# A ConvFFN loop on one NeuronCore: another division of the eight PSUM banks, and another order of VectorE's sums and taps

## The chip, the cores and the metric

The kernel runs on one NeuronCore of a Trainium2 chip. The metric is the device time of one execution in microseconds. Inputs are float32; products on TensorE are made in three passes (high x high, high x low, low x high) so that they keep nearly float32 precision.

## The reference

A two-layer encoder over 1024 tokens of width 1024. Each layer has an attention part (MLA in layer 0, differential attention in layer 1) and then the ConvFFN that the change is about:

```python
def conv_ffn(h, w_up, conv_w, conv_b, w_down):
    u = h @ w_up                       # 1024 x 5632
    u = causal depthwise conv of width 3 over tokens (u) + conv_b
    gate, val = split(u, 2)            # 2816 each
    return (silu(gate) * val) @ w_down
```

The hidden width 2816 is 22 tiles of 128 rows. For every tile there is a gate tile and a value tile of `u` (128 x 1024 tokens), and the down product adds its share to all 8 output tiles.

## The kernel before

The engines run their own instruction lists and meet at semaphores that only count up. `ffn(layer)` exists once per engine.

**One iteration n of the loop (n = 2 to 21; HT = 22, PLAIN = 2).** The gate and the value tile n, each 1024 x 1024 x 128, are made with a Winograd form of the 2x2 block product: seven products P1 to P7 of half size instead of eight. Each product is four steps of three matmuls (L1112 to L1114) into one PSUM bank (128 x 512 float32); a tile pair of the down product, `down(n, f)` (L1117), is six matmuls (L1130 to L1132) into two banks. TensorE's order comes from `tensor_steps` (L73): P1 P6 P2 P5 P7 P4, down tile 0 of n-1, P3, down tiles 1 to 7 of n-1. The first two hidden tiles (n = 0, 1) are made in the plain way, gate in banks 0 and 1, value in banks 2 and 3.

**PSUM.** There are 8 banks. Products of n >= 2 go round banks 0 to 3 (`up_bank`, L535), down tiles alternate between banks 4, 5 and 6, 7 (L1128, L1825). `bank_free` (L1088) makes a product wait until the product that used its bank four products ago has been read: P1 by ScalarE's `bank_copy` (L1191), each other one by the VectorE sum that `RESULT_OF` (L67) names, P7 by C22 and U3. A down tile waits for the sum of the tile two back (`acc_done`, L1124).

**VectorE** (DVE). `result` (L1788) makes the sums of the Winograd form (128 x 512, one input in PSUM): U2 from P6, C11 from P2, W from P5, C22 and U3 from P7, C21 from P4, C12 from P3; C21 completes the value tile, C12 the gate tile (both in `cx`, double buffered). `conv_tile(n, v)` (L1803) adds the two older taps of the convolution (v = 0 gate, v = 1 value) behind ScalarE's `tap` (L1424), which does the newest tap and the bias: two operations of 128 x 1023 and 128 x 1022 with both tensors in SBUF (L1807, L1810). `product` (L1813) multiplies gate and value after ScalarE's Silu (`gate_and_split`, L1430), `hid_tail` (L1818) makes the low part of the result for TensorE, and `add` (L1823) adds one down tile to the accumulator `a`. The order in one iteration:

```python
U2(n); conv_tile(n-1, 1); product(n-1); C11; hid_tail(n-1); W; C22; U3; C21
add(n-1, 0); C12; add(n-1, 1..7); conv_tile(n, 0)
```

**ScalarE** (ACT), in order: `bank_copy(n)`, Silu and high part of n-1, the value's tap (after C21), the gate's tap (after C12 and `hid_tail(n-1)`).

**GpSimd** (POOL) prepares the weights: nine items an iteration (G1 S2 G2 S1 S3 V2 d1 S4 d2, `weight_items`, L89), each a cast (L786) and a subtraction (L788) of 128 x 512, and four weight sums (L797 to L805). The items live in a ring of five slots; `plan_ring` (L118) gives each item the slot that comes free first by the order of TensorE's steps, and the item waits for the step that frees it. SP loads the raw weights: `load_ffn` of V waits for item V2, of G for S4, of D for d2.

Around the start of each FFN (n = 2) P1 and P2 stand ahead of the eight down tiles of n = 0 and wait for the taps of plain tile 1 (gate, value), because those still read the banks.

Of the kernel before, what the change touches and what calls it, by code (L numbers as in the profile page):

```python
# [29 lines left out]
KT = D // P  # L30
# [4 lines left out]
HT = DFF // P  # L35
# [32 lines left out]
PLAIN = 2  # L68
# [4 lines left out]
def tensor_steps():  # L73

    out = [("up", n, c) for n in range(PLAIN) for c in (PARTS if n == 0 else ["g0", "g1", "v0", "v1"])]
    for n in range(PLAIN, HT):
        ups, tiles = [("up", n, c) for c in PRODUCTS], [("dn", n - 1, f) for f in range(KT)]
        if n == PLAIN:
            first = [("up", n, "P1"), ("up", n, "P2")]
            out += first + [("dn", m_, f) for m_ in range(n - 1) for f in range(KT)]  # L80
            ups = [u for u in ups if u not in first]
        if n == HT - 1:
            out += ups + tiles
        else:
            out += ups[:-1] + tiles[:1] + ups[-1:] + tiles[1:]
    return out + [("dn", HT - 1, f) for f in range(KT)]


def weight_items():  # L89

    out = [(n, c) for n in range(PLAIN) for c in ("G1", "G2", "V1", "V2")]
    for n in range(PLAIN, HT):
        if n == PLAIN:
            out += [(n, "G1"), (n, "G2")] + [(m_, c) for m_ in range(n - 1) for c in ("d1", "d2")]
            out += [(n, "S2"), (n, "S1"), (n, "S3")]
        else:
            out += [(n, c) for c in ("G1", "S2", "G2", "S1", "S3")]
        if n == HT - 1:
            out += [(n, "V2"), (n, "S4"), (n - 1, "d1"), (n - 1, "d2")]
        else:  # L100
            out += [(n, "V2"), (n - 1, "d1"), (n, "S4"), (n - 1, "d2")]
    return out + [(HT - 1, "d1"), (HT - 1, "d2")]
# [233 lines left out]
def trunk(nc, xT, W, small, conv, lam_in, cos_in, sin_in, consts, outT):  # L336
    ctx = ExitStack()
    with ctx:
# [83 lines left out]
        def bank(b, n=1):  # L422
            return ps[:, b * HB:(b + n) * HB]
# [109 lines left out]
            return len(RESULTS) * ((HT - PLAIN) * layer + n - PLAIN) + RESULTS.index(name) + 1  # L533

        def up_bank(n, name):  # L535
            return bank((len(PRODUCTS) * (n - PLAIN) + PRODUCTS.index(name)) % 4)

        def conv_count(layer, n, v):
            return 2 * (HT * layer + n) + 1 + v

        def tap_count(layer, n, v):

            return 2 * (HT * layer + n) + 1 + (v if n < PLAIN else 1 - v)

# [298 lines left out]
        def _(pe):  # L843
# [220 lines left out]
            def ffn(layer):  # L1064
                u0 = HT * layer

                def plain(n, part):

                    v, half = int(part[0] == "v"), int(part[1])
                    out = bank(2 * v + half)  # L1070
                    if n:
                        pe.wait_ge(conv_done, conv_count(layer, n - 1, v))
                    for k in range(KT):
                        name = "GV"[v] + "12"[k // KH]
                        if k % KH == 0:
                            pe.wait_ge(item_ready, item_count(layer, n, name))
                        if n == 0:
                            pe.wait_ge(b_lo, 2 * KT * layer + KT * half + k + 1)
                        at_ = ring[RING_SLOT[n, name]]
                        c = k % KH * P  # L1080
                        wh, wl = at_[:, 0, c:c + P], at_[:, 0, HB + c:HB + c + P]
                        xh, xl = direct(half, k)
                        pe.matmul(out, wh, xh, start=k == 0, stop=False)
                        pe.matmul(out, wh, xl, start=False, stop=False)
                        last = pe.matmul(out, wl, xh, start=False, stop=k == KT - 1)
                    last.then_inc(up_done, 1)

                def bank_free(n, place):  # L1088

                    if n == PLAIN and place < 4:  # L1090
                        pe.wait_ge(conv_done, conv_count(layer, n - 1, place // 2))
                        return
                    if place < 4:
                        n, place = n - 1, place + len(PRODUCTS)
                    before = PRODUCTS[place - 4]
                    if before == "P1":
                        pe.wait_ge(bank_copied, (HT - PLAIN) * layer + n - PLAIN + 1)
                    else:
                        pe.wait_ge(c_sum, result_count(layer, n, RESULT_OF[before]))

                def product(n, name):

                    at_ = ring[RING_SLOT[n, WEIGHT_OF[name]]]
                    out, c = up_bank(n, name), TOKENS_OF[name]
                    pe.wait_ge(item_ready, item_count(layer, n, WEIGHT_OF[name]))
                    bank_free(n, PRODUCTS.index(name))
                    for k in range(KH):
                        if n == PLAIN and c[0] == "T":
                            pe.wait_ge(t_rest[c], KH * layer + k + 1)
                        wh, wl = at_[:, 0, k * P:(k + 1) * P], at_[:, 0, HB + k * P:HB + (k + 1) * P]  # L1110
                        _, xh, xl = combination(c, k)
                        pe.matmul(out, wh, xh, start=k == 0, stop=False)  # L1112
                        pe.matmul(out, wh, xl, start=False, stop=False)  # L1113
                        last = pe.matmul(out, wl, xh, start=False, stop=k == KH - 1)  # L1114
                    last.then_inc(up_done, 1)

                def down(n, f):  # L1117
                    part = f // 4
                    at_ = ring[RING_SLOT[n, ("d1", "d2")[part]]]
                    if f % 4 == 0:  # L1120
                        pe.wait_ge(item_ready, item_count(layer, n, ("d1", "d2")[part]))
                        pe.wait_ge(hid_lo, u0 + n + 1)
                    if n > 0 or f >= 2:
                        pe.wait_ge(acc_done, down_count(layer, n, f) - 2)  # L1124
                    f4 = f % 4
                    wh, wl = at_[:, 0, f4 * P:(f4 + 1) * P], at_[:, 0, HB + f4 * P:HB + (f4 + 1) * P]
                    for half in range(2):
                        out = bank(4 + 2 * (f % 2) + half)  # L1128
                        xh, xl = half_of(hid, 2 * (n % 2), half), half_of(hid, 2 * (n % 2) + 1, half)
                        pe.matmul(out, wh, xh, start=True, stop=False)  # L1130
                        pe.matmul(out, wh, xl, start=False, stop=False)  # L1131
                        last = pe.matmul(out, wl, xh, start=False, stop=True)  # L1132
                    last.then_inc(dn_done, 1)

                for sort, n, what in STEPS:
                    if sort == "dn":
                        down(n, what)
                    elif n < PLAIN:
                        plain(n, what)
                    else:  # L1140
                        product(n, what)
# [381 lines left out]
        def _(dve):  # L1523
# [236 lines left out]
            def ffn(layer):  # L1760
# [42 lines left out]
                def conv_tile(n, v):  # L1803
                    u, t = (bank(2 * v, 2) if n < PLAIN else cx[:, 2 * (n % 2) + v, :]), cy[:, v, :]
                    count = conv_count(layer, n, v)
                    dve.wait_ge(tap2, tap_count(layer, n, v))
                    dve.scalar_tensor_tensor(t[:, 1:T], u[:, 0:T - 1], cv[:, 8 * n + 4 * v + 1:8 * n + 4 * v + 2],  # L1807
                                             t[:, 1:T], ALU.mult, ALU.add).then_inc(tap1, 1)
                    dve.wait_ge(tap1, count)
# [12 lines left out]

                def add(n, f):  # L1823
                    dve.wait_ge(dn_done, down_count(layer, n, f))
                    src = bank(4 + 2 * (f % 2), 2)  # L1825
                    if n == 0:
                        dve.tensor_copy(a[:, f, :], src).then_inc(acc_done, 1)
                    else:
                        dve.wait_ge(acc_done, down_count(layer, n - 1, f))
                        dve.tensor_tensor(a[:, f, :], a[:, f, :], src, ALU.add).then_inc(acc_done, 1)  # L1830
# [17 lines left out]
                for f in range(1, KT):  # L1848
                    add(0, f)
                for n in range(PLAIN, HT):  # L1850
                    result(n, "U2")
                    if n > PLAIN:
                        conv_tile(n - 1, 1)
                        product(n - 1)
                    result(n, "C11")
                    hid_tail(n - 1)
# [1 line left out]
                        result(n, name)  # L1858
                    result(n, "C21")
                    if n < HT - 1:  # L1860
                        add(n - 1, 0)
                    result(n, "C12")
                    if n < HT - 1:
                        for f in range(1, KT):
                            add(n - 1, f)
                        conv_tile(n, 0)
                add(HT - 2, 0)
                conv_tile(HT - 1, 0)
                add(HT - 2, 1)
                add(HT - 2, 2)  # L1870
                conv_tile(HT - 1, 1)
                add(HT - 2, 3)
                product(HT - 1)
                add(HT - 2, 4)
# [171 lines left out]
```

## Time and profile before

| | |
|---|---|
| median of 3 runs | 2719.76 us (2710.52 to 2722.84) |
| the profiled execution | 2723.15 us |
| its span, first to last instruction | 2721.4 us |
| TensorE (PE) busy | 2500.6 us, 92% |
| VectorE (DVE) | 1977.5 us, 73% |
| GpSimd (POOL) | 1487.8 us, 55% |
| ScalarE (ACT) | 832.0 us, 31% |
| mean granted TensorE clock | 0.963 of 2.4 GHz |
| the two FFN loops | from about 600 to 1262 us, and from about 2025 to 2687 us |

Times in the rows are microseconds from the start of the span. A matmul is recorded for longer (0.39 us) than it takes in a stream of them; the step from one start to the next tells its cost. In a timeline row the brackets at the end give the idle time of the engine before it and what ended it; "x4" means that four like instructions are merged, and their time is the sum.

### The profile page before, as it was taken

What the parts mean: (1) busy time and instruction counts of PE and PEld (TensorE: products, weight loads), DVE (VectorE), ACT (ScalarE), POOL (GpSimd) and SP (SyncE); (2) the same over time, 40 slices, a digit from 0 to 9 for tenths busy, and PEclk for the clock granted to TensorE, in tenths of its full rate; (3) what the DMA queues carried; (4) which work ended last, traced back from release to release, by engine and by line L of the source; (5) the groups of instructions that cost most, each with busy time, mean ns of one, the idle gap of its engine ahead of it and who ended that gap; (6) DMA issues with size and microseconds to landing.
All of it is one profiled execution on the core that took longest, in us unless ns stands there. A gap on an engine that the chain in (4) does not pass through costs nothing.

```text
span 2721.4 us, 31720 instructions
## 1 busy us (share of the span) xinstructions
PE 2500.6 (92%) x11964; PEld 1975.0 (73%) x11964; DVE 1977.5 (73%) x2181; ACT 832.0 (31%) x1409; POOL 1487.8 (55%) x1153
## 2 busy tenths in 40 slices
PE   6999999879999999996899999979889999999994
PEld 4688888557777777773577787757467777777772
DVE  4466664587888888889656677653687888788888
ACT  3344442241111111113346565651231111111112
POOL 4231212446888888884431323112537888888883
PEclk9999999899999999998899999979989999999997
DMA  3121223111111111113111213042211111111112
GB/s 133 48 76 63 70 94 149 67 62 47 47 48 54 63 47 47 55 39 148 62 49 46 67 56 88 24 155 93 73 51 47 47 55 57 52 47 50 52 62 109
DMA packets 48928, 183.52 MB, mean 67 GB/s; under 512 B 5648, under 2 KB 6160, under 8 KB 45072
## 3 DMA queue, kind: packets, MB, share of 16 engines
q1 hardware_dynamic: 36880, 140.53, 16.1%
q10 hardware_dynamic: 11904, 41.05, 3.9%
q8 instruction: 93, 1.52, 0.2%
q14 instruction: 51, 0.42, 0.0%
HBM read 138.04 MB, written 29.36 MB: 62 GB/s over the span
## 4 chain that ended last, share of the span: by engine, by line
PE 75%; DVE 16%; ACT 4%; issue 2%; DMA 2%; SPq 1%; ACTq 0%; POOL 0%; POOLq 0%; DVEq 0%
PE ps L1112 9%; PE ps L1113 9%; PE ps L1114 9%; PE ps L1130 6%; PE ps L1131 5%; PE ps L1132 5%; PE ps L978 3%; PE ps L876 3%; PE ps L878 3%; PE ps L877 3%; PE ps L950 2%; PE ps L952 2%; DVE a L1554 2%; PE ps L951 2%; PE ps L1015 2%
## 5 line engine op out<-in xcount | busy, mean ns | idle before, releaser
L1830 DVE TENSOR_TENSOR a<-a,ps 128x1024 f32<-128x1024 f32 x336 | 409.4, 1220 | 93.2 <-PE ps L1132 84.3
L705 POOL CAST w_hi<-w_raw 128x1024 fp32r<-128x1024 f32 x62 | 68.1, 1099 | 651.9 <-PE ps L952 275.8
L788 POOL TENSOR_TENSOR ring<-w_raw,ring 128x512 fp32r<-128x512 f32 x216 | 317.8, 1471 | 17.3
L1130 PE MATMUL ps<-hid,ring 128*128 128x512 f32 x704 | 295.1, 419 | 14.1 <-DVE a L1830 12.9
L786 POOL CAST ring<-w_raw 128x512 fp32r<-128x512 f32 x216 | 176.1, 815 | 238.7 <-PE ps L1132 102.3
L1131 PE MATMUL ps<-hid,ring 128*128 128x512 f32 x704 | 278.2, 395 | 0.0
L1132 PE MATMUL ps<-hid,ring 128*128 128x512 f32 x704 | 277.1, 394 | 0.0
L1112 PE MATMUL ps<-h,ring 128*128 128x512 f32 x640 | 253.3, 396 | 22.2 <-DVE cy L1810 22.2
L1801 DVE TENSOR_TENSOR cx<-cx,ps 128x512 f32<-128x512 f32 x280 | 187.7, 683 | 109.9 <-PE ps L1114 101.3
L1113 PE MATMUL ps<-h,ring 128*128 128x512 f32 x640 | 252.2, 394 | 0.0
L1114 PE MATMUL ps<-h,ring 128*128 128x512 f32 x640 | 251.9, 394 | 0.0
L1130 PEld LDWEIGHTS ps<-hid,ring 128*128 128x128 f32 x704 | 132.9, 189 | 100.4 <-DVE a L1830 63.5
L1428 ACT ACTIVATE cy<-cx,cv 128x1024 f32<-128x1024 f32 x80 | 99.7, 1246 | 287.3 <-DVE cx L1801 287.3
L1112 PEld LDWEIGHTS ps<-h,ring 128*128 128x128 f32 x640 | 122.1, 191 | 50.1 <-issue 24.1
L1194 ACT ACTIVATE cx<-ps 128x512 f32<-128x512 f32 x40 | 23.9, 598 | 436.4 <-PE ps L1114 420.5
L1132 PEld LDWEIGHTS ps<-hid,ring 128*128 128x128 f32 x704 | 133.3, 189 | 30.6
L707 POOL TENSOR_TENSOR w_lo<-w_raw,w_hi 128x1024 fp32r<-128x1024 f32 x62 | 151.9, 2450 | 5.0
L788 POOL TENSOR_TENSOR ring<-raw_d,ring 128x512 fp32r<-128x512 f32 x88 | 146.5, 1664 | 7.0
L1131 PEld LDWEIGHTS ps<-hid,ring 128*128 128x128 f32 x704 | 133.5, 190 | 20.5
L876 PE MATMUL ps<-h,w_hi 128*128 128x512 f32 x352 | 139.8, 397 | 8.3 <-POOL h L726 4.3
L1810 DVE SCALAR_TENSOR_TENSOR cy<-cx,cv,cy 128x1022 f32<-128x1022 f32 x80 | 144.9, 1812 | 2.8
L1113 PEld LDWEIGHTS ps<-h,ring 128*128 128x128 f32 x640 | 122.3, 191 | 25.5
(229 smaller groups left out, 6636.8 us busy)
## 6 DMA issues: line engine op xcount, KB each, us to landing
w_raw<-in_W SPq DMA_DIRECT2D x150, 512.0 KB, 3.5
raw_d<-in_W SPq DMA_DIRECT2D x44, 512.0 KB, 3.6
h<-o_dram ACTq DMA_DIRECT2D x2, 6144.0 KB, 21.1
x_dram<-x ACTq DMA_DIRECT2D x6, 2048.0 KB, 7.2
x<-x_dram SPq DMA_DIRECT2D x2, 4096.0 KB, 13.1
dsw<-draw SPq DMA_DIRECT2D x64, 128.0 KB, 2.3
o_dram<-most SPq DMA_DIRECT2D x6, 1024.0 KB, 4.2
o_dram<-dost SPq DMA_DIRECT2D x6, 1024.0 KB, 4.8
```

Of the source, the lines that this page charges most:

```text
L707: pool.tensor_tensor(w_lo[:, slot, :], w_raw[:, slot, :], w_hi[:, slot, :].bitcast(F32), ALU.subtract).then_inc(w_split, 1)
L786: pool.tensor_copy(half_of(at_, 0, 0), raw[name]).then_inc(item_hi, 1)
L788: pool.tensor_tensor(half_of(at_, 0, 1), raw[name], half_of(at_, 0, 0).bitcast(F32), ALU.subtract).then_inc(item_ready, 1)
L876: pe.matmul(out, wh, xh, start=k == 0, stop=False)
L1112: pe.matmul(out, wh, xh, start=k == 0, stop=False)
L1113: pe.matmul(out, wh, xl, start=False, stop=False)
L1114: last = pe.matmul(out, wl, xh, start=False, stop=k == KH - 1)
L1130: pe.matmul(out, wh, xh, start=True, stop=False)
L1131: pe.matmul(out, wh, xl, start=False, stop=False)
L1132: last = pe.matmul(out, wl, xh, start=False, stop=True)
L1801: dve.tensor_tensor(dst, src, up_bank(n, product), ALU.add).then_inc(c_sum, 1)
L1830: dve.tensor_tensor(a[:, f, :], a[:, f, :], src, ALU.add).then_inc(acc_done, 1)
```

## The change

Three parts:

- Banks: products have banks 0 and 1 (each product waits for the reader of the one two back), down tiles have three pairs (2-3, 4-5, 6-7) in turn and wait for the add three tiles back. Down tile 0 of n = 0 also waits for the taps of the plain value tile 1, whose banks it takes over.
- Order at n = 2: only P1 stands ahead of the down tiles of n = 0; P2 goes to its place behind P6, and the weight item G2 behind S2.
- Order on VectorE: in an iteration all eight adds come ahead of C12, and both tap tiles, value first, come behind it, ahead of the next U2. So `conv_done` counts the value tile first (n >= 2), `tap_count` and `conv_count` become one function, and the Silu waits for all four taps.

```diff
--- before.py
+++ after.py
@@ -76,7 +76,7 @@
     for n in range(PLAIN, HT):
         ups, tiles = [("up", n, c) for c in PRODUCTS], [("dn", n - 1, f) for f in range(KT)]
         if n == PLAIN:
-            first = [("up", n, "P1"), ("up", n, "P2")]
+            first = [("up", n, "P1")]
             out += first + [("dn", m_, f) for m_ in range(n - 1) for f in range(KT)]
             ups = [u for u in ups if u not in first]
         if n == HT - 1:
@@ -91,8 +91,8 @@
     out = [(n, c) for n in range(PLAIN) for c in ("G1", "G2", "V1", "V2")]
     for n in range(PLAIN, HT):
         if n == PLAIN:
-            out += [(n, "G1"), (n, "G2")] + [(m_, c) for m_ in range(n - 1) for c in ("d1", "d2")]
-            out += [(n, "S2"), (n, "S1"), (n, "S3")]
+            out += [(n, "G1")] + [(m_, c) for m_ in range(n - 1) for c in ("d1", "d2")]
+            out += [(n, "S2"), (n, "G2"), (n, "S1"), (n, "S3")]
         else:
             out += [(n, c) for c in ("G1", "S2", "G2", "S1", "S3")]
         if n == HT - 1:
@@ -533,12 +533,12 @@
             return len(RESULTS) * ((HT - PLAIN) * layer + n - PLAIN) + RESULTS.index(name) + 1
 
         def up_bank(n, name):
-            return bank((len(PRODUCTS) * (n - PLAIN) + PRODUCTS.index(name)) % 4)
+            return bank((len(PRODUCTS) * (n - PLAIN) + PRODUCTS.index(name)) % 2)
+
+        def down_bank(n, f):
+            return 2 + 2 * ((KT * n + f) % 3)
 
         def conv_count(layer, n, v):
-            return 2 * (HT * layer + n) + 1 + v
-
-        def tap_count(layer, n, v):
 
             return 2 * (HT * layer + n) + 1 + (v if n < PLAIN else 1 - v)
 
@@ -1087,12 +1087,12 @@
 
                 def bank_free(n, place):
 
-                    if n == PLAIN and place < 4:
-                        pe.wait_ge(conv_done, conv_count(layer, n - 1, place // 2))
+                    if n == PLAIN and place < 2:
+                        pe.wait_ge(conv_done, conv_count(layer, n - 1, 0))
                         return
-                    if place < 4:
+                    if place < 2:
                         n, place = n - 1, place + len(PRODUCTS)
-                    before = PRODUCTS[place - 4]
+                    before = PRODUCTS[place - 2]
                     if before == "P1":
                         pe.wait_ge(bank_copied, (HT - PLAIN) * layer + n - PLAIN + 1)
                     else:
@@ -1120,12 +1120,14 @@
                     if f % 4 == 0:
                         pe.wait_ge(item_ready, item_count(layer, n, ("d1", "d2")[part]))
                         pe.wait_ge(hid_lo, u0 + n + 1)
-                    if n > 0 or f >= 2:
-                        pe.wait_ge(acc_done, down_count(layer, n, f) - 2)
+                    if n == 0 and f == 0:
+                        pe.wait_ge(conv_done, conv_count(layer, PLAIN - 1, 1))
+                    if n > 0 or f >= 3:
+                        pe.wait_ge(acc_done, down_count(layer, n, f) - 3)
                     f4 = f % 4
                     wh, wl = at_[:, 0, f4 * P:(f4 + 1) * P], at_[:, 0, HB + f4 * P:HB + (f4 + 1) * P]
                     for half in range(2):
-                        out = bank(4 + 2 * (f % 2) + half)
+                        out = bank(down_bank(n, f) + half)
                         xh, xl = half_of(hid, 2 * (n % 2), half), half_of(hid, 2 * (n % 2) + 1, half)
                         pe.matmul(out, wh, xh, start=True, stop=False)
                         pe.matmul(out, wh, xl, start=False, stop=False)
@@ -1803,7 +1805,7 @@
                 def conv_tile(n, v):
                     u, t = (bank(2 * v, 2) if n < PLAIN else cx[:, 2 * (n % 2) + v, :]), cy[:, v, :]
                     count = conv_count(layer, n, v)
-                    dve.wait_ge(tap2, tap_count(layer, n, v))
+                    dve.wait_ge(tap2, count)
                     dve.scalar_tensor_tensor(t[:, 1:T], u[:, 0:T - 1], cv[:, 8 * n + 4 * v + 1:8 * n + 4 * v + 2],
                                              t[:, 1:T], ALU.mult, ALU.add).then_inc(tap1, 1)
                     dve.wait_ge(tap1, count)
@@ -1822,7 +1824,7 @@
 
                 def add(n, f):
                     dve.wait_ge(dn_done, down_count(layer, n, f))
-                    src = bank(4 + 2 * (f % 2), 2)
+                    src = bank(down_bank(n, f), 2)
                     if n == 0:
                         dve.tensor_copy(a[:, f, :], src).then_inc(acc_done, 1)
                     else:
@@ -1848,9 +1850,11 @@
                 for f in range(1, KT):
                     add(0, f)
                 for n in range(PLAIN, HT):
+                    if n > PLAIN:
+                        conv_tile(n - 1, 1)
+                        conv_tile(n - 1, 0)
                     result(n, "U2")
                     if n > PLAIN:
-                        conv_tile(n - 1, 1)
                         product(n - 1)
                     result(n, "C11")
                     hid_tail(n - 1)
@@ -1858,17 +1862,14 @@
                         result(n, name)
                     result(n, "C21")
                     if n < HT - 1:
-                        add(n - 1, 0)
+                        for f in range(KT):
+                            add(n - 1, f)
                     result(n, "C12")
-                    if n < HT - 1:
-                        for f in range(1, KT):
-                            add(n - 1, f)
-                        conv_tile(n, 0)
                 add(HT - 2, 0)
-                conv_tile(HT - 1, 0)
+                conv_tile(HT - 1, 1)
                 add(HT - 2, 1)
                 add(HT - 2, 2)
-                conv_tile(HT - 1, 1)
+                conv_tile(HT - 1, 0)
                 add(HT - 2, 3)
                 product(HT - 1)
                 add(HT - 2, 4)
```

## Rows read from the trace of the kernel before

**Rows 1.** Windows: stretch, us; busy (count) of PE, PEld, DVE, ACT, POOL; clock; DMA.

```profile
1000.00:1100.00 100.00, 100.00 (x432) 79.64 (x431) 82.40 (x68) 16.70 (x16) 87.62 (x71) 1.00 0.17 53
1230.00:1260.00 30.00, 23.40 (x85) 16.13 (x84) 29.76 (x27) 9.77 (x9) 6.76 (x4) 0.94 0.33 140
1234.59:1238.00 3.41, 3.41 (x9) 2.63 (x10) 3.37 (x3) 0.00 (x0) 0.00 (x0) 0.54 0.85 365
1532.90:1536.00 3.10, 3.10 (x14) 2.57 (x15) 2.55 (x4) 0.77 (x2) 0.00 (x0) 1.00 0.00 0
```

**Rows 2.** Timeline of TensorE in one iteration: start, duration, engine, line, operation.

```profile
900.99 0.39 PE L1112 MATMUL ps<-h,ring 128*128 128x512 f32 x1
...
909.17 0.39 PE L1112 MATMUL ps<-h,ring 128*128 128x512 f32 x1
...
917.33 0.39 PE L1130 MATMUL ps<-hid,ring 128*128 128x512 f32 x1
...
924.25 0.50 PE L1130 MATMUL ps<-hid,ring 128*128 128x512 f32 x1
...
931.70 0.39 PE L1112 MATMUL ps<-h,ring 128*128 128x512 f32 x1
```

**Rows 3.** The view of line L1130 (us, times), and the waits view of TensorE.

```profile
  DVE a L1830: 76.4, 184
...
PE ps L1112 <- DVE cy L1810: 22.2, 4, 6.4
```

**Rows 4.** Timeline of VectorE, one iteration, and a tap near the loop's end.

```profile
931.90 1.22 DVE L1830 TENSOR_TENSOR a<-a,ps 128x1024 f32<-128x1024 f32 x1 [0.37 <-PE ps L1132]
933.04 1.95 DVE L1807 SCALAR_TENSOR_TENSOR cy<-cx,cv,cy 128x1023 f32<-128x1023 f32 x1
935.02 1.51 DVE L1810 SCALAR_TENSOR_TENSOR cy<-cx,cv,cy 128x1022 f32<-128x1022 f32 x1
937.37 0.69 DVE L1801 TENSOR_TENSOR cx<-cx,ps 128x512 f32<-128x512 f32 x1 [0.83 <-PE ps L1114]
...
941.66 2.13 DVE L1816 TENSOR_TENSOR cy<-cy 128x1024 f32<-128x1024 f32 x1
...
944.91 1.80 DVE L1820 TENSOR_TENSOR hid<-cy,hid 128x1024 fp32r<-128x1024 f32 x1 [0.53 <-ACT hid L1434]
...
1235.60 1.27 DVE L1807 SCALAR_TENSOR_TENSOR cy<-cx,cv,cy 128x1023 f32<-128x1023 f32 x1
```

**Rows 5.** Timeline of TensorE at the start of layer 0's FFN.

```profile
612.56 0.77 PE L1112 MATMUL ps<-h,ring 128*128 128x512 f32 x1 [5.93 <-DVE cy L1810]
...
617.46 0.40 PE L1130 MATMUL ps<-hid,ring 128*128 128x512 f32 x1
...
630.04 0.39 PE L1112 MATMUL ps<-t_r,ring 128*128 128x512 f32 x1
```

**Rows 6.** Timeline of GpSimd in the same iteration.

```profile
932.62 1.28 POOL L788 TENSOR_TENSOR ring<-w_raw,ring 128x512 fp32r<-128x512 f32 x1
934.67 0.78 POOL L786 CAST ring<-w_raw 128x512 fp32r<-128x512 f32 x1 [0.77 <-PE ps L1114]
935.54 2.16 POOL L788 TENSOR_TENSOR ring<-w_raw,ring 128x512 fp32r<-128x512 f32 x1
...
938.34 2.13 POOL L788 TENSOR_TENSOR ring<-raw_d,ring 128x512 fp32r<-128x512 f32 x1
940.44 2.26 POOL L805 TENSOR_TENSOR w_raw<-w_raw,s 128x512 f32<-128x512 f32 x1
```

**Rows 7.** Timeline of ScalarE: the value's tap, and a Silu.

```profile
922.33 1.25 ACT L1428 ACTIVATE cy<-cx,cv 128x1024 f32<-128x1024 f32 x1 [2.27 <-DVE cx L1801]
...
936.57 1.06 ACT L1432 ACTIVATE cy<-cy 128x1024 f32<-128x1024 f32 x1 [1.33 <-DVE cy L1810]
```

**Rows 8.** Timeline of TensorE: first matmuls behind two long idles.

```profile
1532.90 0.50 PE L950 MATMUL ps<-h,w_hi 128*128 128x512 f32 x1 [1.71 <-DVE dt L1648]
...
1234.59 0.61 PE L1130 MATMUL ps<-hid,ring 128*128 128x512 f32 x1 [2.85 <-DVE a L1830]
```

## The prediction

> **What bounds the kernel now.** The windows view comes first. Over 100 us in the middle of a ConvFFN loop TensorE is busy without a break at the full clock, VectorE 82 us and GpSimd 88 us [rows 1]. So TensorE sets the end there, but its busy time can hide slow matmuls, so I read starts, not ends. In the loop the product P1 starts at 900.99 and again at 931.70: one iteration lasts 30.71 us and holds 7x12 + 8x6 = 132 matmuls. From P5 (909.17) to the first down tile (917.33) 36 matmuls take 8.16 us, 0.227 us each [rows 2]. 132 of them need 29.95 us, so 0.76 us of each iteration is lost. The lost time sits in the down tiles: the tile at 924.25 begins with a matmul of 0.50 instead of 0.39 us [rows 2], and the view of the line says what held the tiles: the sums "DVE a L1830", 184 times, 76.4 us with the weight load's own waiting [rows 3]. A tile pair is written while the other is being added; an add takes 1.22 us [rows 4], a tile 6x0.227 = 1.36 us, and what lies between the end of one and the start of the other eats the 0.14 us of difference.
>
> The second loss is at the start of each FFN: TensorE waits four times, 22.2 us in all, for the taps of the two plain tiles (L1112 <- L1810) [rows 3]. In layer 0 P2 starts only at 612.56, and runs slowly until the down tiles begin at 617.46; those end at 630.04, when P6 starts [rows 5].
>
> **The change part by part.**
>
> *Three pairs for down tiles.* A tile waits for the add three tiles back, not two: the slack is 0.14 + 1.36 us, against a loss of at most 0.11 us a restart and some 0.1 us a wait. I take the stall as gone: -0.76 us per iteration in 19 iterations (n = 2 to 20) of each layer. Bounds: 0 (the stall stays) and -0.76. The next thing that could hold a tile is VectorE's rate, 1.22 against 1.36 us, and it does not. At the FFN's end (the tiles of n = 20 and 21) VectorE is busy 29.8 of 30 us [rows 1]; its work there is the same, only the two tap tiles change places, so 0.
>
> *The plain part.* The banks of the value tile go to the down tiles, so now P1 stands ahead of the wait, and the down tiles of n = 0 wait for the tap that P2 waited for. That wait costs the same. Behind it are the same 60 matmuls. They now take 17.48 us (612.56 to 630.04) [rows 5]; without stalls it is the 4.90 us of the first twelve, most of them slow, and 48 x 0.227 = 10.9: 15.8. Gain 1.7 us a layer. P2 moves behind P6, item G2 behind S2, and two ring slots (of S3 and V2) come free with down tiles 3 and 7 instead of P2 and tile 3. On GpSimd's queue an item takes 3.0 us even where it is hindered (934.67 to 935.54 + 2.16) [rows 6], and S3 and V2 are used three and four products of 2.7 us behind P6. SP's load of the next V waits for V2; its first reader stands behind item d2, which waits for P5, again 8 us later. So 0; without that cover up to 2 us a layer.
>
> *The order on VectorE and two banks for products.* This is the costly part. With two banks, P5 needs the bank of P6, so it waits for U2(n); P7 waits for C11, P4 for W, P6 for C12 of the iteration before. And U2 now stands behind both tap tiles of n-1, all of which stand behind the eight adds and C12. Before, only the gate tile's two taps lay there, and U2 started in time, when P6 had ended. I lay it out from t = 0, the first matmul of P1 (931.70).
> - The last add runs from 0.20 to 1.42 [rows 4], then C12 (0.69 like U2, starting 0.08 before the add ends) to 2.03. P6 is due at 2.72: no stall.
> - Four taps follow. They read two SBUF tensors, and beside GpSimd they take turns: the tap of 933.04 ends 1.09 us after GpSimd's operation of 932.62; the cast of 934.67 ends 0.46 after that tap; the next tap 1.08 after the cast; the subtraction of 935.54 1.17 after that [rows 4, 6]. GpSimd's work is bound to TensorE's steps (idle until P1 ends, 934.67), so it falls on the same microseconds. The first tap waits for the subtraction that ends at 2.20: 2.20 + 1.09 (tap) = 3.29; + 0.46 (cast of V2) + 1.08 (tap) = 4.83; + 1.17 (subtraction) + 1.09 (tap) = 7.09; + 0.46 (cast of d1) + 1.08 (tap) = 8.63. The gate's tap on ScalarE (from 2.03, 1.25 us [rows 7]) is done long before its turn.
> - U2 ends at 8.63 - 0.08 + 0.69 = 9.24. P5 is due at 909.17 - 900.99 = 8.18. So TensorE stands 1.06 us, and with the way through the semaphore and the slow first matmul (0.11) 1.2 us.
> - Then the product of gate and value. It needs the Silu, which now waits for the last tap: 8.66 to 9.72 (1.06 us [rows 7]). GpSimd has its subtraction of d1 until 8.63 + 1.14 = 9.77 and its next operation, the weight sum of L805, is issued 0.03 before that (940.44 against 938.34 + 2.13) [rows 6]: 9.74. The product is issued at 9.75. Both ask for the same access at practically the same moment. If the product is served first it ends at 10.9, C11 at 11.6, P7 is due at 12.1: no more stalls, and the iteration takes 29.95 + 1.2 = 31.15 us. If the weight sum is served first, the product ends at 12.05, C11 at 12.7, P7 stands 0.6 us and restarts (0.1); hid_tail (1.80 [rows 4]) and W end at 15.6, and P4 stands another 0.1 and restarts: 32.1 us in all.
>
> GpSimd is ahead by about 0.01 us, less than my rounding; I take the middle, as if each order came in half of the iterations: 31.6 us, +0.9 against 30.71. Ends: +0.44 and +1.39. Everything behind P4 has its slack.
>
> **The sum.** Per layer: 18 iterations (n = 3 to 20) x 0.9 = +16.2; n = 21, whose end is VectorE's, still has the stalls ahead of it, +1.2 to +2.1, 1.65; the plain part -1.7; the tiles of n = 2, -0.76. Together +15.4, for two layers +30.8. The profiled execution took 2723.15 us around its span of 2721.4, which is 3.4 over the median of 2719.76; so 2754 against it, and some 2751 as a median. All at one end: 2737 less 3 = 2733, or 2772 less 3 = 2769.
>
> **A rule against the trace.** A TensorE idle of 1.71 us is followed by 0.5 and then ordinary matmuls, 14 started in 3.1 us at a granted clock of 1.00 (2.4 GHz); behind an idle of 2.85 us nine start in 3.4 us at 0.54, most of it at 1.2 GHz [rows 8, 1]. The new stall of 1.2 us is nearer the first, so the sum has no clock term. The Trainium skill, page "TensorE: Matmul & The Clock Gate", section "A second HAM failure mode: psum-queue depth-cycling", warns that short idles as a kernel cycles through its PSUM banks can bring the clock down again and again; the trace, with its stalls at down tiles and a clock of 1.00 all through the loop, does not agree so far.
>
> **The rivals.**
> - *The product is always served first* (the short order): 2733. Nothing in the trace decides the order. With the opposite one, 2769. These are the two ends of my own case: 0.72 for the three together, of which 0.2 for the short order alone.
> - *Faster: the taps run nearly unhindered.* If GpSimd's three operations between 2.95 and 7.6 fell elsewhere, four taps of 1.27 (1235.60, no GpSimd beside it [rows 4]) would end at about 7.1 and U2 at 7.7, ahead of P5's 8.18. Then the gain of 0.76 stays: 18 x 0.76 + 0.76 + 1.7 = 16.1 a layer, 2688. It decides at a shortening of 1.1 us. Against it: GpSimd is busy 88% and its release points (P1, P6) are fixed to TensorE. 0.10.
> - *The clock falls behind each stall.* Each then costs as the one at 1234.59: nine starts in 3.41 instead of 15, 6 x 0.227 = 1.4 us; 38 of them, 52 us: 2803. For it: the new idle is ten times one of the old. Against it: rows 8. 0.06.
> - *The tiles stall as before*, though three pairs are there (an add that is late for another reason, C12 or tap included): the 0.76 is not won, 2751 + 2 x 19 x 0.76 = 2780. 0.05.
> - *It is near nothing*: stalls hidden by something that I don't see, between 2706 and 2733. 0.07.
>
> **The numbers.** A measurement of this kernel can tell about 0.5% (13.6 us) from no change: 2706 and 2733 are the bounds. Faster is the second rival, 0.10. Same takes the last one, and of the short order, which lies on the bound, most: 0.07 + 0.15 = 0.22. Slower 0.68. The range reaches from 2718, inside "near nothing", to 2778, above the long order.
>
> **What the profile will show.** Right: an iteration of 31.1 to 32.1 us; no idle at L1130 in the loop; TensorE waits at L1112 for "DVE cx L1801" about 38 times by 1.0 us (P5 behind U2), and if the long order holds another 38 times for C11; the product of L1816 near 1.25 us where it goes first, near 2.3 us where not (2.1 now, row of 941.66 [rows 4]); GpSimd's waits for TensorE longer by what TensorE stands; the four taps at 6.6 us together; granted clock 1.00 in the loop. Wrong: U2 starting when P6 ends, waits for L1801 at P6 (C12 late), or a clock under 1.00.

## The result, and the profile after

The changed kernel takes **2775.7 us** (median of 5 runs, 2771.6 to 2779.3) against 2719.7 us (5 runs, 2710.5 to 2722.8): the ratio is 1.021, with an interval of 1.0196 to 1.0224. It is 56 us slower. The profiled execution took 2774.61 us around a span of 2772.8.

Busy time and the chain that ended last, from the page after:

```profile
PE 2481.6 (89%) x11964; PEld 1973.7 (71%) x11964; DVE 1972.0 (71%) x2181; ACT 827.6 (30%) x1409; POOL 1491.2 (54%) x1153
...
PE 58%; DVE 29%; ACT 5%; issue 4%; DMA 2%; SPq 1%; ACTq 0%; POOL 0%; POOLq 0%; DVEq 0%
```

The instruction counts are the same. In the chain of before PE had 75% and DVE 16%: VectorE now stands on the path in the loop. Two stretches in the windows view (columns as in [rows 1]):

```profile
650.00:1200.00 550.00, 523.85 (x2258) 419.51 (x2257) 424.31 (x360) 86.56 (x85) 456.09 (x375) 1.00 0.15 49
1000.00:1100.00 100.00, 95.32 (x413) 76.49 (x412) 77.23 (x66) 15.28 (x15) 83.31 (x70) 1.00 0.15 48
```

The second answers to the first of [rows 1]: TensorE now stands 4.7 us in 100. The clock is 1.00 over the loop, so none of the loss is a clock. What TensorE waits for, from the waits view (us, times, longest) and from the view of line L1132, the first matmul of a down tile:

```profile
PE ps L1112 <- DVE cx L1803: 58.7, 74, 1.7
PE ps L1112 <- DVE cy L1812: 22.3, 2, 11.2
...
PE ps L1132 <- DVE a L1832: 10.2, 12, 1.7
```

```profile
  DVE a L1832: 23.4, 24
```

The 184 idles of [rows 3] at down tiles are 24, and the 12 of them that are the matmuls' own (the other 12 are those of the weight loads) all lie at the end of the two FFNs, six in each. The third pair does what it was to do. In its place stand 74 waits of products for VectorE's results: 38 of P5 and 36 of P7. One iteration on TensorE, the counterpart of [rows 2] (P1, P5, P7, P4, first down tile, next P1; P6 to C22 and U3 in between have no idle):

```profile
911.79 0.39 PE L1112 MATMUL ps<-h,ring 128*128 128x512 f32 x1
...
921.16 0.47 PE L1112 MATMUL ps<-h,ring 128*128 128x512 f32 x1 [1.05 <-DVE cx L1803]
...
924.63 0.47 PE L1112 MATMUL ps<-x_r,ring 128*128 128x512 f32 x1 [0.50 <-DVE cx L1803]
...
927.56 0.47 PE L1112 MATMUL ps<-x_r,ring 128*128 128x512 f32 x1
...
930.40 0.39 PE L1132 MATMUL ps<-hid,ring 128*128 128x512 f32 x1
...
944.00 0.39 PE L1112 MATMUL ps<-h,ring 128*128 128x512 f32 x1
```

It lasts 32.21 us. VectorE in the same iteration, the counterpart of [rows 4]:

```profile
913.13 0.68 DVE L1803 TENSOR_TENSOR cx<-cx,ps 128x512 f32<-128x512 f32 x1
913.73 1.36 DVE L1809 SCALAR_TENSOR_TENSOR cy<-cx,cv,cy 128x1023 f32<-128x1023 f32 x1
915.13 1.51 DVE L1812 SCALAR_TENSOR_TENSOR cy<-cx,cv,cy 128x1022 f32<-128x1022 f32 x1
916.56 2.31 DVE L1809 SCALAR_TENSOR_TENSOR cy<-cx,cv,cy 128x1023 f32<-128x1023 f32 x1
918.91 1.51 DVE L1812 SCALAR_TENSOR_TENSOR cy<-cx,cv,cy 128x1022 f32<-128x1022 f32 x1
920.35 0.67 DVE L1803 TENSOR_TENSOR cx<-cx,ps 128x512 f32<-128x512 f32 x1
921.55 2.35 DVE L1818 TENSOR_TENSOR cy<-cy 128x1024 f32<-128x1024 f32 x1 [0.53 <-ACT cy L1434]
923.82 0.67 DVE L1803 TENSOR_TENSOR cx<-cx,ps 128x512 f32<-128x512 f32 x1
925.02 1.80 DVE L1822 TENSOR_TENSOR hid<-cy,hid 128x1024 fp32r<-128x1024 f32 x1 [0.53 <-ACT hid L1436]
926.74 0.68 DVE L1803 TENSOR_TENSOR cx<-cx,ps 128x512 f32<-128x512 f32 x1
```

The first row is C12, then come the four taps, U2 (920.35), the product of gate and value, C11 (923.82), hid_tail and W. Each time the product that needs the bank starts 0.14 us after one of them ends: P5 at 921.16 behind U2 (to 921.02), P7 at 924.63 behind C11 (to 924.49), P4 at 927.56 behind W (to 927.42). P4's row shows no idle, because a matmul is recorded for longer than it takes; but it starts 2.93 us behind P7, where 2.72 is the time of a product. And GpSimd beside the product, the counterpart of the last two of [rows 6]:

```profile
919.42 2.13 POOL L788 TENSOR_TENSOR ring<-raw_d,ring 128x512 fp32r<-128x512 f32 x1
921.52 1.29 POOL L805 TENSOR_TENSOR w_raw<-w_raw,s 128x512 f32<-128x512 f32 x1
```

The weight sum starts 0.03 us ahead of the product and runs in 1.29 us, unhindered; the product takes 2.35. It is so in all 36 iterations from n = 3 to 20: by the two timelines the weight sum starts 0.02 to 0.03 us ahead each time, and the product takes 2.34 to 2.36. The view of the product's line (min, median, max in ns; the short ones lie at the start and the end of the FFNs):

```profile
L1818 DVE TENSOR_TENSOR cy<-cy x44: 1215/2344/2355, 581.4 to 2715.3; 128x1024 f32<-128x1024 f32 x44
```

**Where the 56 us went.** All of this is read from the two profiled executions. P1 of n = 3 and of n = 21 start at 655.32 and 1208.19 before, at 654.20 and 1233.63 after: 18 iterations of 30.71 and of 32.19 us, +26.6 in layer 0. The products of n = 21 go from 19.06 to 21.47 us (+2.4; the first idle there, at P5, is 1.74 long), the tail from its first down tile to the end of the FFN from 41.44 to 40.42 (-1.0). From the FFN's first plain matmul (548.41 before, 546.86 after) to P1 of n = 3 it is 106.91 and 107.34 (+0.4). That is +28.4 in layer 0. In layer 1, from its FFN's first matmul (1973.16 and 1997.26) to the end of the span, it is 748.2 and 775.5: +27.3. What lies ahead of and between the FFNs, where nothing was changed, was 1.6 and 2.7 us shorter in this execution; together that is the 51.4 us between the two spans.

### The profile page after: what moved, and what is told of

It reads as the page before. It is cut to its first block, busy times and chain, and to the rows that moved or that the text cites. A ratio compares the mean times of both kernels' runs of the same rounds, so it can differ in the third digit from the quotient of the medians.

```text
span 2772.8 us, 31720 instructions
## 1 busy us (share of the span) xinstructions
PE 2481.6 (89%) x11964; PEld 1973.7 (71%) x11964; DVE 1972.0 (71%) x2181; ACT 827.6 (30%) x1409; POOL 1491.2 (54%) x1153
## 3 DMA queue, kind: packets, MB, share of 16 engines
q1 hardware_dynamic: 36880, 140.53, 15.8%
## 4 chain that ended last, share of the span: by engine, by line
PE 58%; DVE 29%; ACT 5%; issue 4%; DMA 2%; SPq 1%; ACTq 0%; POOL 0%; POOLq 0%; DVEq 0%
DVE cy L1809 5%; PE ps L1132 5%; PE ps L1134 5%; PE ps L1133 5%; PE ps L1112 5%; DVE cy L1812 5%; PE ps L1114 4%; PE ps L1113 4%; DVE cy L1818 3%; PE ps L978 3%; PE ps L876 3%; PE ps L878 3%; PE ps L877 3%; PE ps L950 2%; DVE a L1556 2%
## 5 line engine op out<-in xcount | busy, mean ns | idle before, releaser
L1132 PE MATMUL ps<-hid,ring 128*128 128x512 f32 x704 | 277.7, 394 | 17.1 <-DVE a L1832 10.2
L1133 PE MATMUL ps<-hid,ring 128*128 128x512 f32 x704 | 275.6, 392 | 0.0
L1134 PE MATMUL ps<-hid,ring 128*128 128x512 f32 x704 | 275.5, 391 | 0.0
L1132 PEld LDWEIGHTS ps<-hid,ring 128*128 128x128 f32 x704 | 133.2, 189 | 51.9 <-DVE a L1832 13.3
L1133 PEld LDWEIGHTS ps<-hid,ring 128*128 128x128 f32 x704 | 133.3, 189 | 27.3
L1112 PE MATMUL ps<-x_r,ring 128*128 128x512 f32 x320 | 131.2, 410 | 17.4 <-DVE cx L1803 17.4
L1809 DVE SCALAR_TENSOR_TENSOR cy<-cx,cv,cy 128x1023 f32<-128x1023 f32 x80 | 144.8, 1810 | 0.0
```

## The experiments

The theory: with two banks for products, P5, P7 and P4 start when VectorE has served U2, C11 and W, and these stand behind four taps, which take turns with GpSimd. The rivals that I tested against it: the new order of VectorE alone costs the time (more collisions with GpSimd); the two banks alone cost it, whatever the order; the product's turn behind the weight sum has no part in it.

**e1, the banks of the change with VectorE's order of before** (against the changed kernel; the lines that set back the counts and the two tap tiles at the FFN's end are left out)

```diff
-                    if n > PLAIN:
-                        conv_tile(n - 1, 1)
-                        conv_tile(n - 1, 0)
                     result(n, "U2")
                     if n > PLAIN:
+                        conv_tile(n - 1, 1)
                         product(n - 1)
...
-                        for f in range(KT):
-                            add(n - 1, f)
+                        add(n - 1, 0)
                     result(n, "C12")
+                    if n < HT - 1:
+                        for f in range(1, KT):
+                            add(n - 1, f)
+                        conv_tile(n, 0)
```

> The changed kernel (two banks for products, three pairs for down tiles) with VectorE's order of before. Theory (two product banks tie TensorE to how early VectorE serves U2, C11 and W): U2 comes in time, but C11 stands behind the value's taps and the product of gate and value, as it did at 12.7 us behind P1's start, while P7 is due at 10.9. So the stall moves from P5 to P7, about 1.8 us plus 0.1 twice for restarts, and the iteration again takes about 32.0 us: 2770 to 2780 us. Rival (the order alone is the cost: taps behind the adds): the stall is gone and the three pairs give their 0.76 us, 29.95 us an iteration, about 2690 us.

Measured: 2788.9 us (2787.5 to 2789.3), ratio to before 1.0261 (1.0244 to 1.0278); 2718.2 for before, run beside it. So the old order with two banks is worse than the new one. The waits view:

```profile
PE ps L1115 <- DVE cx L1806: 68.5, 38, 1.8
```

And TensorE's timeline (P7 in a usual iteration; P7 of n = 21 in layer 0, with the matmuls behind it):

```profile
927.35 0.47 PE L1115 MATMUL ps<-x_r,ring 128*128 128x512 f32 x1 [1.80 <-DVE cx L1806]
...
1255.00 0.50 PE L1115 MATMUL ps<-x_r,ring 128*128 128x512 f32 x1 [1.82 <-DVE cx L1806]
1255.30 0.62 PE L1116 MATMUL ps<-x_r,ring 128*128 128x512 f32 x1
1255.72 0.63 PE L1117 MATMUL ps<-x_r,ring 128*128 128x512 f32 x1
1256.15 0.63 PE L1115 MATMUL ps<-x_r,ring 128*128 128x512 f32 x1
```

P5 is in time now, because U2 (920.15) stands ahead of the last two taps; but C11 stands behind them and the product (2.13 us here), and P7 waits 1.8 us for it, 38 times. A usual iteration is 32.20 us, as in the changed kernel. But in 9 of the 36 iterations from n = 3 to 20 the matmuls behind the idle start 0.43 us apart, not 0.23, for some nine of them, and the iteration takes 33.6; the same happens at P7 of n = 21 in both layers, so behind 11 of the 38 idles. Windows view of one such place, and of the loop:

```profile
1255.00:1258.71 3.71, 3.71 (x10) 2.93 (x10) 2.38 (x2) 0.34 (x1) 3.63 (x3) 0.54 0.00 0
...
650.00:1200.00 550.00, 519.36 (x2227) 421.01 (x2226) 424.32 (x355) 87.35 (x84) 451.66 (x372) 0.98 0.16 49
```

The granted clock is at 1.2 GHz for most of these 3.7 us. The nine iterations cost 9 x 1.4 = 12.6 us and the two at n = 21 some 2 us more; the medians of e1 and the changed kernel are 13.2 us apart. So the mechanism is the theory's, and the clock, which it did not have, accounts for the 9 us by which e1 lies above the 2770 to 2780 that I had expected.

**e2, the new order of VectorE with the banks of before** (against the kernel before; the counts and the end of the FFN are left out again)

```diff
+                    if n > PLAIN:
+                        conv_tile(n - 1, 1)
+                        conv_tile(n - 1, 0)
                     result(n, "U2")
                     if n > PLAIN:
-                        conv_tile(n - 1, 1)
                         product(n - 1)
...
-                        add(n - 1, 0)
-                    result(n, "C12")
-                    if n < HT - 1:
-                        for f in range(1, KT):
+                        for f in range(KT):
                             add(n - 1, f)
-                        conv_tile(n, 0)
+                    result(n, "C12")
```

> The kernel of before (four banks for products, two pairs for down tiles) with VectorE's order of the change alone. Theory: with four banks P5 waits for C12 of the iteration before, P7 for the bank copy, P4 for U2, P3 for C11, all in time; the down tiles stall as before (0.76 us): 30.7 us an iteration, 2715 to 2725 us. Rival (the order costs by itself, since U2 and the product come later): an iteration over 31 us, 2740 us or more.

Measured: 2721.9 us (10 runs, 2715.8 to 2725.6), ratio 1.0013 (1.0003 to 1.0023); the iteration is 30.73 us. The view of the down tile's line:

```profile
  DVE a L1827: 77.9, 183
```

VectorE's timeline (U2, product, C11):

```profile
941.07 0.68 DVE L1798 TENSOR_TENSOR cx<-cx,ps 128x512 f32<-128x512 f32 x1
942.28 2.36 DVE L1813 TENSOR_TENSOR cy<-cy 128x1024 f32<-128x1024 f32 x1 [0.53 <-ACT cy L1429]
944.56 0.68 DVE L1798 TENSOR_TENSOR cx<-cx,ps 128x512 f32<-128x512 f32 x1
```

U2 and C11 come as late as in the changed kernel and the product takes its 2.36 us, yet no product waits: with four banks the results have the length of two more products in hand. The late order costs next to nothing by itself (a ratio of 1.0013), and the 0.76 at the down tiles is back. The two banks are what costs: 56 us with the new order, 71 with the old one (e1). Whether they cost in any order is the question of e3.

**e3, the new banks, and VectorE serving C11 ahead of the product and W ahead of hid_tail** (against e1)

```diff
                         conv_tile(n - 1, 1)
-                        product(n - 1)
                     result(n, "C11")
+                    if n > PLAIN:
+                        product(n - 1)
+                    result(n, "W")
                     hid_tail(n - 1)
-                    for name in ("W", "C22", "U3"):
+                    for name in ("C22", "U3"):
```

> Banks of the change, VectorE's order of before with C11 ahead of the product of gate and value and W ahead of hid_tail. Theory: each sum that frees a bank is over before the product that needs it is due (U2 at 6.4, C11 at about 10.5 against P7's 10.9, W at about 13.3 against P4's 13.6), so no product stalls and the down tiles have three pairs: 132 x 0.227 = 29.95 us an iteration. Against before 19 x 0.76 us a layer less, the plain part +0.4 to +1.2 as in the changed kernel: 2690 to 2697 us. Rival (two banks for products are too few in any order): some 0.5 us or more of stall stays in each iteration, 2715 us or more.

Measured: 2687.7 us (2685.3 to 2689.2), ratio 0.9889 (0.9872 to 0.9906), 30.5 us under before and 2 us under the range that I had expected. The windows view of the loop:

```profile
650.00:1200.00 550.00, 550.00 (x2428) 455.44 (x2427) 452.00 (x386) 95.49 (x92) 488.54 (x403) 1.00 0.16 52
```

VectorE's timeline (U2 at 926.94, C11 at 931.09, W at 933.32):

```profile
926.94 0.69 DVE L1806 TENSOR_TENSOR cx<-cx,ps 128x512 f32<-128x512 f32 x1 [0.80 <-PE ps L1117]
...
931.09 0.68 DVE L1806 TENSOR_TENSOR cx<-cx,ps 128x512 f32<-128x512 f32 x1
931.69 1.71 DVE L1821 TENSOR_TENSOR cy<-cy 128x1024 f32<-128x1024 f32 x1
933.32 0.67 DVE L1806 TENSOR_TENSOR cx<-cx,ps 128x512 f32<-128x512 f32 x1
```

TensorE has not one idle in 550 us, and 2428 matmuls in them where the changed kernel has 2258. The iteration is 29.92 us, which is 132 x 0.2267: nothing is left to win in it but matmuls. So two banks are enough if the results are served in the order in which the banks come due; C11 ends at 931.77 and P7 starts at 932.18. Less the 0.14 us from a result's end to the matmul that waited for it, some 0.3 us are the room.

**e4, the changed kernel with the weight sum L805 moved into GpSimd's idle time ahead of P1**

```diff
-                    elif name == "S4":
+                    item(n, name)
+                    if n > PLAIN and name == "S1":
                         last_sum(n)
-                    item(n, name)
+                    if n == PLAIN and name == "V2":
+                        last_sum(n)
```

> The changed kernel with one move on GpSimd: the weight sum for S4 (L805) is made behind item S1, where GpSimd waited for TensorE, not behind item d1, where it asks for access together with the product of gate and value. Theory (the long order: the product of 2.34 us is behind that sum): now at most a cast (0.46 us) is ahead of it, the product takes some 1.7 us, C11 is over when P7 is due, and only the stall of P5 stays: 31.2 us an iteration, 2738 to 2748 us. Rival (the product is slow for another reason, or the stall of P7 comes from the taps): no change, 2770 to 2780 us.

Measured: 2748.6 us (2746.1 to 2752.0), ratio 1.0118 (1.0101 to 1.0135); the iteration is 31.43 us. The waits view, and below it the product on VectorE's timeline:

```profile
PE ps L1114 <- DVE cx L1805: 42.5, 38, 1.1
```

```profile
944.68 1.65 DVE L1820 TENSOR_TENSOR cy<-cy 128x1024 f32<-128x1024 f32 x1 [0.52 <-ACT cy L1436]
```

The 74 waits are 38: P5's stays, P7's is gone, and the product is 1.65 us instead of 2.35. That is 27 us of the 56, and it shows that the weight sum's turn is the cause of the second stall. It is 0.6 us over the range that I had expected, and 0.3 us an iteration more than the 31.15 of the short order: the cast that comes next on GpSimd still meets the product (1.65, not 1.1 us), and P5 starts 1.28 us behind its due time of 8.16, and 1.21 in the changed kernel; the matmuls from P5 to P4 lose 0.2 us more in small steps (29.92 + 1.28 + 0.23 = 31.43).

**e6, the order of e3 with the banks of before** (the same edit of VectorE's loop, in the kernel before)

> The kernel of before with VectorE's order of e3 (C11 ahead of the product, W ahead of hid_tail), its banks and pairs as before. Theory (the gain of e3 is the third pair; the order only lets it be had with two product banks): as before, 2714 to 2723 us, with the down tiles' stall in every iteration. Rival (the order is a gain by itself): below 2710 us.

Measured: 2719.1 us (10 runs, 2715.0 to 2721.2), ratio 1.0003 (0.9991 to 1.0015), the iteration 30.67 us. The view of the down tile's line:

```profile
  DVE a L1830: 78.5, 186
```

With four banks for products the better order is worth nothing, and the down tiles stall as before. e3's kernel, run beside this one (e3b below), is 29.5 us faster, and 36 x (30.67 - 29.92) = 27 us of that is the stall at the down tiles that the third pair takes away. A kernel with three pairs and four product banks can't be had, since it would need ten banks.

**e5 and e3b, the plain part.** The weight sums of n = 2 (L797 to L801) stand ahead of item S2. With G2 moved behind S2, item d2 ahead of them no longer waits for its ring slot (it waited 5.57 us before), and the sums run some 9 us earlier (from 589.14, not 598.40). e5 is e3 with a wait ahead of them; e3b is e3 once more, beside it:

```diff
                     if n >= PLAIN and name == ("S2" if n == PLAIN else "G1"):
+                        if n == PLAIN:
+                            pool.wait_ge(up_done, up_count(layer, PLAIN - 1, "v1"))
                         sums(n)
```

> The kernel of e3 with one wait more on GpSimd: at n = 2 the three weight sums (L797 to L801) wait until the plain value tile 1 is done on TensorE, as they did before the change, where item d2 ahead of them waited for it. Theory: in the changed kernel and in e3 these sums moved some 8 us earlier and take turns with VectorE's sums and rests of the Winograd inputs (four rests in 6.2 us instead of 2.5, four sums in 5.0 instead of 2.5), so the value's taps end 2.2 us later behind the FFN's first matmul; with the wait they end 2 to 4 us earlier, in both layers: 4 to 8 us less than e3. Rival: other work fills the time, 0 to 1 us.

> The kernel of e3 again, on the same chip as e5, as its base: 2683 to 2692 us by every theory.

Measured: e5 2683.6 us (2681.8 to 2688.3), ratio 0.9883 (0.9866 to 0.9899); e3b 2689.5 (2688.5 to 2692.3), ratio 0.9902 (0.9886 to 0.9919). VectorE's timeline ahead of the last taps, in e3b:

```profile
588.64 6.18 DVE L1791 TENSOR_TENSOR h<-a,h 128x512 fp32r<-128x512 f32 x4
594.75 5.03 DVE L1785 TENSOR_TENSOR a<-a,cx 128x512 f32<-128x512 f32 x4
```

and in e5:

```profile
588.88 2.48 DVE L1793 TENSOR_TENSOR h<-a,h 128x512 fp32r<-128x512 f32 x4
591.29 2.48 DVE L1787 TENSOR_TENSOR a<-a,cx 128x512 f32<-128x512 f32 x4
```

TensorE's first down tile, in e3b and in e5:

```profile
611.65 0.48 PE L1135 MATMUL ps<-hid,ring 128*128 128x512 f32 x1 [1.87 <-DVE cy L1815]
```

```profile
609.70 0.77 PE L1137 MATMUL ps<-hid,ring 128*128 128x512 f32 x1 [6.32 <-DVE cy L1817]
```

The eight operations ahead of the taps take 4.9 us instead of 11.1. The last plain matmul starts at 592.75 in e3b and at 592.97 in e5, so the down tiles begin 18.9 and 16.7 us behind it: 2.2 us in layer 0, and as much in layer 1. That is 4.4 of the 5.9 us between the medians; the rest I cannot place, and unchanged code differs by as much between two executions. e5 is the fastest version: 1.2% under the kernel before.

## Why the prediction was right, and where it was off

The direction and the range held, and so did the mechanism laid out for the loop; the number was 25 us low, and the measured 2775.7 lies only 2 us inside the range's upper end. The forecast was 31 us slower, the result is 56. By its steps:

- **The clock.** As predicted, 1.00 in the loop after.
- **Three pairs.** Right: no idle at a down tile in the loop, and e3 shows the gain where no product stalls: 30.71 less 29.92 is 0.79 us, predicted 0.76.
- **The layout of an iteration.** It held to some hundredths. From t = 0 at 911.79, with the predicted values in brackets: taps end 8.63 (8.63), U2 9.23 (9.24), P5 starts 9.37 after an idle of 1.05 (1.06), the weight sum is issued at 9.73 and the product at 9.76 (9.74 and 9.75), the product ends at 12.11 (12.05), C11 at 12.70 (12.7), P7's idle is 0.50 (0.6), W ends at 15.63 (15.6). The iteration is 32.2; the long order was worked out to 32.1. Behind the taking of turns the Trainium skill has a rule: its page "SBUF — State Buffer", section "SBUF: two separate sides", says that a VectorE operation with two SBUF inputs and a GpSimd operation that reads SBUF exclude each other, and that the one that starts first keeps the ports to its end. The trace agrees: the product of 2.35 us ends 1.09 us behind the weight sum, and the weight sum's 1.29 is not longer than where nothing stands beside it (1.28).
- **The tie: the term that was mis-sized.** Between the product and the weight sum I "took the middle, as if each order came in half of the iterations": 31.6. There is no half. The weight sum's lead of 0.03 us is there in the next iteration again (953.72 against 953.75), and in all 36 of them it is 0.02 to 0.03 us. That both hang on one chain from P1 is my reading of why it repeats. A lead that is small is not therefore random. With the long order throughout, the working gave 2769; against that the result is 7 us off. e4 puts the tie, both layers together, at 27 us.
- **n = 21.** Predicted +1.65, with +2.1 as its upper end; +2.4 measured. The idle at P5 is 1.74 and 1.73 us there, not 1.05: in the last iteration GpSimd has the weight sum (1239.60, 2.27 us) ahead of item d1, so it is the last tap that comes behind it (1240.75, 2.20 us instead of 1.51), and U2 ends 0.7 us later. The working had the same four taps for n = 21 as for the loop.
- **The plain part.** The largest other miss: predicted -1.7, and -0.76 for the tiles of n = 2; measured +0.4 in layer 0. The tiles' gain came (from P6 to P1 of n = 3 it is 25.28 us before, 27.20 less P2's 2.72, so 24.48 after). The 60 matmuls behind the wait took 613.18 to 627.00 and P2's 2.72, 16.5 us, not 15.8, because the first fourteen start 0.43 us apart here too. And the down tiles begin 2.2 us later after the FFN's start than P2 did. I had costed the moved items at 0, asking who waits for them, and named 2 us as the price without that cover. The cover that failed was another: not a reader that waits, but VectorE, with which the weight sums, now earlier, take turns. e3b against e5 shows it.
- **The tail.** Predicted 0, measured -1.0.

In sum, per layer: +15.4 predicted; +10.4 from the loop (9.0 of it the tie, 18 x 0.5; the rest is 32.19 against the 32.1 worked out, and rounding), +0.75 from n = 21, +2.9 from the plain part and -1.0 from the tail make 28.4. The two large misses, the tie and the plain part, both made the forecast too low; only the tail's 1.0 went the other way.

**The rivals.** The short order alone falls by the product's row; e4 comes near it, 2749 where 2733 was worked out; the 0.3 us an iteration and the plain part make most of the difference. Unhindered taps fall: they took 6.69 us, and the first three end at 3.30, 4.85 and 7.08 where 3.29, 4.83 and 7.09 were laid out. The clock that falls behind each stall is not seen in the changed kernel; e1 has it behind 11 of its 38 idles, which are 1.80 to 1.82 us long. Tiles that stall as before: none in the loop. The Trainium skill, page "TensorE: Matmul & The Clock Gate", section "A second HAM failure mode: psum-queue depth-cycling", warns of a clock that falls again and again as banks are cycled through. The changed kernel's loop does not bear it out (clock 1.00), and e1's does in part (0.98).

A version with the weight sum and the order of e3 both moved was not tried. Why the clock fell behind 11 idles of e1 and not behind the other 27 is open.

## What to carry to other kernels

Moving PSUM banks from one producer to another moves a deadline: with two banks for products instead of four every result had to be read two products earlier, so rewrite the evicting engine's order first (here the order in which VectorE serves its queue made the same banks cost 2.1% or save 1.1%), and lay out one iteration from the operation that all of it hangs on. When such a layout ends in a tie between two engines, forecast both ends and not their mean: in this loop the tie fell the same way in all 36 iterations. And when an item is moved in a queue, look not only at who waits for it but at what will now run beside it.

## What the runs showed of the hardware that was not expected

- A lead of 0.02 to 0.03 us decided between VectorE and GpSimd, and for the whole operation: 1.29 us for the one, 2.35 for the other (1.65 in e4, where a cast of 0.61 is in the way). VectorE's sums with an input in PSUM were never held up: in the changed kernel those of 128x512 took 0.67 to 0.69 us, all 280 of them.
- The clock after a short idle. In e1 idles of 1.80 to 1.82 us were followed by matmuls at half the clock in 11 cases of 38, at a cost of 1.4 us in each of the nine in the loop. In the changed kernel idles of 1.05 us (36) and of 1.73 and 1.74 us (one each) never were, nor were the 38 of 1.12 us in e4. My nearest row for "no clock term", an idle of 1.71 us [rows 8], was right for 1.2 us. It would not have served for e1, whose idle is only 0.1 us longer.
